# A hybrid encoder trunk on one core: norm sums of squares inside the output projections, roots with tokens on partitions, and one convolution operation per tap

## The chip, the cores and the metric

The kernel runs on one core of a Trainium2 chip. The metric is device time in microseconds (us) of one execution; the time of a kernel is the median of its runs.

## What is computed

Four layers act on a residual stream x of 768 tokens (a prompt of 512 and a sample of 256, independent streams that share weights) with 1024 channels, in fp32. Layers 0 and 3 mix with RWKV-7, layer 1 with Hyena long convolutions, layer 2 with a Conformer convolution module; a final norm ends the trunk.

```python
def rmsnorm(x, g):
    y = xf * lax.rsqrt(jnp.mean(xf * xf, axis=-1, keepdims=True) + RMS_EPS)
    return (y * g).astype(x.dtype)
def conformer_conv_mixer(h, w_in, dw_w, dw_b, ln_g, ln_b, w_out):
    a, b, g = jnp.split(h @ w_in, 3, axis=-1)
    u = a * jax.nn.sigmoid(b)
    u = depthwise_conv(u, dw_w, dw_b)              # 31 taps, per channel
    u = jax.nn.silu(layernorm(u, ln_g, ln_b))
    return (u * jax.nn.silu(g)) @ w_out
def trunk(...):
    for i in range(DEPTH):
        shift, scale, gate = ...                   # from silu(c) @ mod_w[i] + mod_b[i]
        hn = rmsnorm(x, norm_g[i]) * (1 + scale) + shift
        o = mixer(hn)                              # ends in @ w_out
        x = x + (gate * o)
    return rmsnorm(x, final_g)
```

## The kernel before

Channels lie on the 128 partitions, in eight tiles of 128 (KT = 8, index k or j); tokens lie along the free dimension, in two halves of 384 (h = 0 and 1). BX holds the residual, BH the normed input h, BD the residual times the root's inverse (and later scratch), BY the gated mixer output, SQ two 768-column scratch tiles. PSUM has eight banks: PJ (0, 1) for products, SC (2, 3), and IV, IU, SQB, YB (4 to 7). Each engine has its own program, written by hand and in order; semaphores join them.

A layer runs so. The **norm** (`norm` on PE, ACT and DVE): ACT squares each of the eight tiles (L1342), PE multiplies each square by a 128x128 matrix of 1/1024 (MEAN), which sums over channels and spreads the sum over all partitions (L982, 8 x 2 products of 384 columns); ACT takes the root of 768 columns (L1347), DVE its reciprocal (L1917), then x times it for eight tiles (BD, L1925); ACT scales and shifts into BH (L1357), a piece for the prompt and a piece for the sample. Before its first square, ACT waits for the last store of the residual to DRAM. Then comes the **mixer**. Its first weights and constants are loaded by SP after the whole of BH is there in layers 1 and 2; in layers 0 and 3 DVE first builds shifted differences of all of BH (L1945 to L1949). Then the **output projection** (`out_act`, `out_dve`, and the loop on PE, L949): eight products of 16 matmuls each, back to back on PE; DVE adds each to the old residual (L1433), which ACT has brought from DRAM two tiles at a time into SQ, and ACT stores the new one.

In layer 0 the norm stands beside the first modulation rounds on PE (`mod_rounds`, L627), which wait for 512 KB weight loads.

In the **conformer** PE makes three products a channel tile (slots b, a, g, in that order, banks CB[0] to CB[2], one buffer each); ACT takes a tanh of b and of g; DVE makes the gated input CU (L1649), then the gate BY (L1655), then 31 taps (L1668, L1671), each one operation for the prompt's 512 columns and one for the sample's 256, and a closing operation into BD (L1674).

Of the kernel before, what the change touches and what calls it, by code (L numbers as in the profile page):

```python
# [17 lines left out]
D = 1024  # L18
# [36 lines left out]
NV_CF = CONV + 3  # L55
NV_HY = 14
# [53 lines left out]
PER = {"act": {"gate": 0}, "dve": {"mod": 0, "gates": 0, "gate": 0, "pair": 73, "hy": 188, "cf": 64, "out": 0}}  # L110


def trunk_program(nc, a, out, layers=(0, 1, 2, 3)):
# [9 lines left out]
    with ctx:  # L123
# [18 lines left out]
        XO = SQ  # L142
# [12 lines left out]
        SEL = sb("SEL", [P, 2])  # L155

# [37 lines left out]
        CACC = own("CACC", [P, 2, T])  # L194
# [18 lines left out]
        alone.close()  # L213

# [22 lines left out]
        xn_ready, h_ready, hn_done = sem("xn_ready"), sem("h_ready"), sem("hn_done")  # L237
# [71 lines left out]
        for l in layers:  # L309
            phase((l, "norm"), 0, (), 1)  # L310
# [14 lines left out]
        phase(("final", "norm"), 0, (), 1)  # L325
# [70 lines left out]
        def tiles_hy(sp, l, load, free, cols):  # L396
# [3 lines left out]
            def one(j, first):  # L400
# [3 lines left out]
                for s, grp in enumerate((2, 0, 1, 3)):  # L404
                    load(s, cols(a["hy_w_in"][0], j + grp * KT), free[s] if first else (pj_full[1], j * 4 + (base + s - 3)))
                    if first and s == 0:
                        sp.wait_ge(h_ready, KT * (NRM[l] + 1))
# [18 lines left out]
        def _(sp):  # L426
# [30 lines left out]
            for l in layers:  # L457
                if l % 3 == 0:
# [16 lines left out]
                    def pair(j, first):  # L475
# [5 lines left out]
                        else:  # L481
                            sp.wait_ge(h_ready, KT * (NRM[l] + 1))
# [17 lines left out]
                if l % 3 == 2:  # L500
# [5 lines left out]
                    sp.wait_ge(h_ready, KT * (NRM[l] + 1))  # L506
# [289 lines left out]
        def pe_hyena(pe, l, product, weights, done):  # L796
# [4 lines left out]
            def project(j, s, halves=(0, 1)):  # L801
                weights((l, "hy"), s, j)
                for h in halves:
                    pe.wait_ge(pj_free[h], j * 4 + (base + s + 1))
                    for k in range(KT):
                        if type(j) is int and j == 0 and s == 0 and h == 0:
                            pe.wait_ge(h_ready, KT * NRM[l] + k + 1)
# [129 lines left out]
        def _(pe):  # L937
            pe.sem_inc(sq_used, 2)
# [32 lines left out]

            def norm(l):

                n, prods = NRM[l], plan[(l, "norm")][1]
                if n == 0:
                    pe.wait_ge(const_ready, 176)
                for k in range(KT):
                    pe.wait_ge(sq_ready, n * KT + k + 1)
                    for h in range(2):
                        if k == 0:  # L980
                            pe.wait_ge(pj_free[h], prods + 1)
                        mm = pe.matmul(pj(h), MEAN, SQ[:, k % 2, tok(h)], start=(k == 0), stop=(k == KT - 1))  # L982
                    mm.then_inc(sq_used, 1)

                pe.wait_ge(sq_used, n * KT + KT + 2)
                pe.sem_inc(pj_full[0], 1)
                pe.sem_inc(pj_full[1], 1)
# [5 lines left out]
            for l in layers:  # L993
                norm(l)
                if l == layers[0]:
                    pe.wait_ge(sc_ready, 1)
                    mod_rounds("mod", 0, MOD_FIRST)
# [23 lines left out]
                if l % 3 == 2:  # L1021
                    for j in range(0, KT):
                        for s in range(3):
                            weights((l, "cf"), s, j)
                            for h in range(2):

                                pe.wait_ge(cb_free[s][h], j + 1)
                                for k in range(KT):
                                    if s == 0 and h == 0:
# [1069 lines left out]
```

## Time and profile before

| | us |
|---|---|
| time, median of 3 runs (4233.78 to 4238.66) | 4234.78 |
| the profiled execution's own time | 4246.76 |
| its span, first to last instruction | 4245.0 |
| PE busy in it | 3499.3 (82%) |
| DVE busy | 2101.5 (50%) |
| ACT busy | 1136.3 (27%) |

The profiled execution is one run, 0.28% above the median. In the chain of work that ended last, followed back from the last instruction, PE has 31% of the span, DVE 9%, waiting that the profile doesn't explain 6%, ACT 1%, DMA under 1%. The mean granted TensorE clock is 0.895 of its full 2.4 GHz.

### The profile page before, as it was taken

Reading aid. Unit: us, or ns where it says so; the run is one execution under the profiler, and the core shown is the slowest. Engines: PE = TensorE matmul, PEld = TensorE weight load, DVE = VectorE, ACT = ScalarE, POOL = GpSimd, SP = SyncE. Lnnn points to the kernel's source line nnn. Section 1 sums busy time; section 2 is a strip of 40 time slices with the busy share of each in tenths; the row PEclk is TensorE's granted clock in tenths of the full one; section 3 lists DMA queues with packets and bytes.
Section 4 is the critical chain, followed back from the end, with each engine's and each line's share of the span. In section 5 each row is a group of like instructions: output and inputs, shape, how many; then the busy total and the mean of one; then the engine's idle time right before and its main releaser. Section 6 shows DMA issues by size and latency. Waiting matters only on the chain. (4 is left out here: it accounts for less than half of the span.)

```text
span 4245.0 us, 96984 instructions
## 1 busy us (share of the span) xinstructions
PE 3499.3 (82%) x41452; PEld 2472.3 (58%) x41452; DVE 2101.5 (50%) x4017; ACT 1136.3 (27%) x2764; POOL 0.2 (0%) x4
## 2 busy tenths in 40 slices
PE   4978888889888859899979797387788888888977
PEld 2556766676676526666655454144466666766664
DVE  3253454354444235767761599613545544454432
ACT  2132333333233113333320200101233333333320
POOL 0000000000000000000000000000000000000000
PEclk7989998888898979999989898698899989989988
DMA  3111111110110211111102111020000000000002
GB/s 141 55 62 41 54 45 34 48 63 27 38 62 32 88 69 32 38 30 45 30 20 80 51 45 45 8 92 30 27 18 8 18 17 13 13 13 18 16 24 93
DMA packets 65781, 178.67 MB, mean 42 GB/s; under 512 B 9104, under 2 KB 22544, under 8 KB 65424
## 3 DMA queue, kind: packets, MB, share of 16 engines
q1 hardware_dynamic: 53472, 144.02, 10.2%
q10 hardware_dynamic: 11952, 29.04, 1.9%
q8 instruction: 328, 5.37, 0.5%
q14 instruction: 29, 0.24, 0.0%
HBM read 157.30 MB, written 15.73 MB: 41 GB/s over the span
## 5 line engine op out<-in xcount | busy, mean ns | idle before, releaser
L1624 DVE SCALAR_TENSOR_TENSOR RBF<-bank,ID 128x256 bf16<-128x256 f32 x480 | 194.0, 423 | 402.7 <-PE bank L610 396.4
L949 PE MATMUL bank<-BY,W 128*128 128x384 f32 x1024 | 340.4, 496 | 48.0 <-DVEq L1697 35.3
L808 PE MATMUL bank<-BH,W 128*128 128x384 f32 x1024 | 341.6, 489 | 6.9 <-ACT HZ L1210 6.6
L949 PEld LDWEIGHTS bank<-BY,W 128*128 128x128 f32 x1024 | 198.7, 195 | 188.4 <-DVEq L1697 35.9
L1031 PE MATMUL bank<-BH,W 128*128 128x384 f32 x768 | 261.4, 505 | 38.2 <-DMA W<-in_cf_w_in 22.9
L949 PE MATMUL bank<-BX,W 128*128 128x384 f32 x640 | 219.1, 500 | 66.4 <-DVE BX L1936 66.1
L808 PEld LDWEIGHTS bank<-BH,W 128*128 128x128 f32 x1024 | 191.3, 191 | 136.3 <-issue 15.5
L1671 DVE SCALAR_TENSOR_TENSOR CACC<-CU,CV,CACC 128x512 f32<-128x512 f32 x480 | 254.7, 611 | 0.0
L1031 PEld LDWEIGHTS bank<-BH,W 128*128 128x128 f32 x768 | 151.2, 198 | 148.3 <-issue 29.8
L771 PE MATMUL bank<-BD,W 128*128 128x384 f32 x512 | 228.5, 575 | 0.0
L730 PE MATMUL bank<-BH,W 128*128 128x384 f32 x512 | 213.0, 546 | 8.9 <-DVE BH L1936 8.9
L949 PEld LDWEIGHTS bank<-BX,W 128*128 128x128 f32 x640 | 121.2, 193 | 163.7 <-issue 71.3
L1433 DVE SCALAR_TENSOR_TENSOR BX<-bank,MOD,SQ 128x384 f32 (+2 forms) x96 | 43.5, 481 | 301.0 <-PE bank L949 235.4
L730 PE MATMUL bank<-BX,W 128*128 128x384 f32 x512 | 181.2, 498 | 0.0
L610 PE MATMUL bank<-LN,Z 64*64 64x64 f32 x4608 | 163.7, 221 | 3.8 <-issue 3.8
L610 PEld LDWEIGHTS bank<-LN,Z 64*64 64x64 f32 x4608 | 149.0, 136 | 23.4 <-issue 23.4
L662 PE MATMUL bank<-VT,KS 64*64 64x64 f32 x1536 | 110.9, 239 | 44.7 <-ACTq L1133 26.6
L1342 ACT ACTIVATE SQ<-BX 128x768 f32<-128x768 f32 x40 | 33.2, 843 | 410.1 <-DMA x_scratch<-BX 376.1
L553 PE MATMUL bank<-BK,AR 64*64 64x64 f32 x1536 | 75.1, 268 | 73.8 <-DVE BK L1595 38.7
L1634 DVE TENSOR_TENSOR Z<-Z,bank 128x256 f32<-128x256 f32 x288 | 109.6, 418 | 52.8 <-PE bank L620 50.7
L730 PEld LDWEIGHTS bank<-BH,W 128*128 128x128 f32 x512 | 96.6, 204 | 66.3 <-issue 24.4
L620 PEld LDWEIGHTS bank<-ZB,RBF 64*64 64x64 bf16 x3840 | 95.0, 109 | 57.1 <-issue 52.7
(264 smaller groups left out, 6476.1 us busy)
## 6 DMA issues: line engine op xcount, KB each, us to landing
W<-in_mod_w SPq DMA_DIRECT2D x96, 512.0 KB, 3.6
W<-in_rw_w_in SPq DMA_DIRECT2D x68, 512.0 KB, 3.7
W<-in_hy_w_in SPq DMA_DIRECT2D x32, 512.0 KB, 7.0
x_scratch<-BX ACTq DMA_DIRECT2D x32, 384.0 KB, 3.4
W<-in_cf_w_in SPq DMA_DIRECT2D x24, 512.0 KB, 3.4
SQ<-x_scratch ACTq DMA_DIRECT2D x24, 384.0 KB, 4.2
W<-in_rw_w_out SPq DMA_DIRECT2D x16, 512.0 KB, 3.7
W<-in_hy_w_out SPq DMA_DIRECT2D x8, 512.0 KB, 3.5
```

The lines of the kernel that those rows point to most:

```text
L553: mm = pe.matmul(SC[1][rows, (d * GC + c) * CH:(d * GC + c + 1) * CH], AR[rows, p, d, c, 0, :], BK[rows, d, c, 0, :], start=True, stop=True)
L610: mm = pe.matmul(NB[d][rows, c * CH:(c + 1) * CH], lhs, rhs, start=True, stop=True)
L620: mm = pe.matmul(NB[d][rows, GT + c * CH:GT + (c + 1) * CH], RBF[rows, d, c, :], ZB[rows, d, c, :], start=True, stop=True)
L662: mm = pe.matmul(SQB[rows, o], KS[rows, p, d, c, 0, :], VT[rows, SGS[s][d] * GC + c, :], start=True, stop=not state)
L730: mm = pe.matmul(pj(h), W[:, s, k, :], src[:, k, tok(h)], start=(k == 0), stop=(k == KT - 1))
L771: mm = pe.matmul((SQB, YB)[h][:, 0:HALF], W[:, 2, k, :], BD[:, k, tok(h)], start=(k == 0), stop=(k == KT - 1))
L808: mm = pe.matmul(pj(h), W[:, s, k, :], BH[:, k, tok(h)], start=(k == 0), stop=(k == KT - 1))
L949: mm = pe.matmul(pj(h), lhs(k), rhs(k, h), start=(k == 0), stop=(k == nk - 1))
L1031: mm = pe.matmul(CB[s][h][:, 0:HALF], W[:, s, k, :], BH[:, k, tok(h)], start=(k == 0), stop=(k == KT - 1))
L1624: v.scalar_tensor_tensor(RBF[:, d, :, :], xout(d), -1.0, bc(ID2[:, 1 if r < NBF else 0, :], GC), ALU.mult, ALU.add).then_inc(ir_ready, 1)
L1634: v.tensor_tensor(z, z, uout(d), ALU.add).then_inc(z_ready, 1)
L1671: ins = v.scalar_tensor_tensor(dst, src, w, dst, ALU.mult, ALU.add)
```

## The change

In every output projection ACT squares each residual tile as DVE finishes it, a half at a time, and PE sums the squares there: for a square tile it loads each 128-token piece as the weights and multiplies it by one column of MEAN, so that the sums come out with tokens on partitions, three columns a half in SC. Each tile's sums follow the next tile's product in PE's order. The norm that follows takes roots and reciprocals of 128x3 elements a half (RN), lays them out as a diagonal pattern (RX, then SQ), and one product a half with MEAN spreads them over the partitions into SQB and YB. DVE's multiply into BD and ACT's scaling into BH then go by halves, with semaphores counted a half. The old residual comes into a buffer of its own (XOUT: TW, HZ or CACC by layer), two tiles ahead; a square root of one element at the start of the projection has ACT's table loaded there; the wait for the last store stands ahead of BH. In layer 0 the sums are taken up front, and PE's first modulation rounds wait until all of BD is made.

In the conformer a tap is one operation over 798 columns (both streams and the padding between them), in two accumulators in turn, which a closing pair of operations adds. The halving that the closing operation did is put into the tap weights once. The gate is made ahead of tap 12.

```diff
             with C.loop("cf", KT) as j:
...
+            C.link(v.tensor_scalar(CVA[:, :, 0:CONV], CVA[:, :, 0:CONV], 0.5, None, ALU.mult))
...
                 for tap in range(CONV):
-                    for st, (t0, ln) in enumerate(STREAMS):
-                        src = CU[:, starts[st] - PADW + tap:starts[st] - PADW + tap + ln]
-                        dst = CACC[:, 0, t0:t0 + ln]
-                        w = CV[:, tap:tap + 1]
-                        if tap == 0:
-                            ins = v.tensor_scalar(dst, src, w, None, ALU.mult)
-                        else:
-                            C.wait(last[st])
-                            ins = v.scalar_tensor_tensor(dst, src, w, dst, ALU.mult, ALU.add)
-                        last[st] = C.mark(ins)
+                    if tap == GATE_TAP:
+                        for h in range(2):
+                            v.wait_ge(cf_tanh, j * 2 + h + 1)
+                            v.scalar_tensor_tensor(BY[:, bass.ds(j, 1), tok(h)].squeeze(1), TT[:, 1, tok(h)], 1.0, CB[2][h][:, 0:HALF],
+                                                   ALU.add, ALU.mult).then_inc(cb_free[2][h], 1)
+                    b = tap % 2
+                    src, dst, w = CU[:, tap:tap + T + 2 * PADW], CACC[:, b, :], CV[:, tap:tap + 1]
+                    if tap < 2:
+                        ins = v.tensor_scalar(dst, src, w, None, ALU.mult)
+                    else:
+                        C.wait(last[b])
+                        ins = v.scalar_tensor_tensor(dst, src, w, dst, ALU.mult, ALU.add)
+                    last[b] = C.mark(ins)
...
+            def squares(n, k):
+                for h in range(2):
+                    pe.wait_ge(sq_ready, n * 2 * KT + 2 * k + h + 1)
+                    for c in range(3):
+                        t = h * HALF + c * P
+                        mm = pe.matmul(SC[h][:, c:c + 1], SQ[:, k % 2, t:t + P], MEAN[:, 0:1], start=(k == 0 and c == 0), stop=(k == KT - 1 and c == 2))
+                    mm.then_inc(sq_used, 1)
             def norm(l):
-                for k in range(KT):
-                    pe.wait_ge(sq_ready, n * KT + k + 1)
...
+                for h in range(2):
+                    pe.wait_ge(dg_ready, n * 2 + h + 1)
+                    pe.matmul((SQB, YB)[h][:, 0:HALF], MEAN, SQ[:, 0, tok(h)], start=True, stop=True).then_inc(r_full, 1)
...
                         done(product(i * 4 + (base + s), lambda k: W[:, s, k, :], lambda k, h: BY[:, k, tok(h)], KT), s)
+                        if i * 4 + s:
+                            squares(NRM[l] + 1, i * 4 + s - 1)
+                squares(NRM[l] + 1, KT - 1)
...
+            act.activation(RN[:, 0, 0:1], EPSV[:, 0:1], ACT.Sqrt)
+            for j in range(-2, KT):
+                if j >= 0:
                     for h in range(2):
                         act.wait_ge(pj_free[h], j + (base + 2))
+                        act.wait_ge(sq_used, (n + 1) * 2 * KT + 2 * j + h + 1)
+                        act.activation(SQ[:, j % 2, tok(h)], BX[:, j, tok(h)], ACT.Square).then_inc(sq_ready, 1)
+                    act.dma_start(a["xs"][n][j * P:(j + 1) * P, :], BX[:, j, :]).then_inc(x_out, 16)
+                if j + 2 < KT:
+                    act.dma_start(xo[:, j % 2, 0:T], src[(j + 2) * P:(j + 3) * P, :]).then_inc(xo_in[j % 2], 16)
...
+                    act.activation(RN[:, h, :], SC[h][:, 0:3], ACT.Sqrt, bias=EPSV[:, 0:1]).then_inc(rt_ready, 1)
...
+                        for k in range(KT):
+                            act.wait_ge(xn_ready, n * 2 * KT + h * KT + k + 1)
+                            for t0, t1, st in (((0, HALF, 0),) if h == 0 else ((HALF, LP, 0), (LP, T, 1))):
...
-                C.link(v.reciprocal(RS[:, :], RS[:, :]))
+                    v.wait_ge(rt_ready, n * 2 + h + 1)
+                    C.link(v.reciprocal(RN[:, h, :], RN[:, h, :]))
+                    C.link(v.scalar_tensor_tensor(RX[:, h, :, :], bc(RN[:, h, :], 2, 2), float(D), bc(HSUM[:, 0:P:HEAD], 3), ALU.mult, ALU.mult))
+                    v.tensor_tensor(SQ[:, 0, tok(h)].rearrange("p (x e) -> p x e", e=HEAD), bc(RX[:, h, :, :].rearrange("p c x -> p (c x)"), HEAD, 2),
+                                    bc(ID2[:, 0, :], 6), ALU.mult).then_inc(dg_ready, 1)
```

How PE's order moves is seen at the end of layer 1 and the start of layer 2. Before, PE's program there has Hyena's last inverse transform (INV), the output projection (BY with weights W), the norm's sums (SQ with the constant matrix K) and the conformer's input products (BH):

```order
L837 MATMUL bank<-INV,UP 128x128 x12
L949 MATMUL bank<-BY,W 128x384 x128
L982 MATMUL bank<-SQ,K 128x384 x16
L1031 MATMUL bank<-BH,W 128x384 x384
L949 MATMUL bank<-BD,K 128x384 x16
```

Now, at the end of the same projection (its first two products, 32 matmuls, stand ahead of the first six sums, and each later product of 16 is followed by six):

```order
L950 MATMUL bank<-BY,W 128x384 x16
L979 MATMUL bank<-K,SQ 128x1 x6
L950 MATMUL bank<-BY,W 128x384 x16
L979 MATMUL bank<-K,SQ 128x1 x12
L991 MATMUL bank<-SQ,K 128x384 x2
L1036 MATMUL bank<-BH,W 128x384 x384
```

The sixteen 384-column sums became 48 one-column ones, of which 36 stand inside the projection and 12 behind it, and two 384-column products are left between those and the next layer.

DVE's order in the conformer's loop, for one channel tile, was this before (CU the gated input, BY the gate, CACC the accumulator; two more operations for each of the 30 later taps):

```order
L1649 SCALAR_TENSOR_TENSOR CU<-SQ,bank 128x256
L1654 ISA
L1655 ISA
L1655 SCALAR_TENSOR_TENSOR BY<-SQ,bank 128x384
L1654 REGISTER_ALU
L1655 ISA
L1655 SCALAR_TENSOR_TENSOR BY<-SQ,bank 128x384
L1668 TENSOR_SCALAR CACC<-CU,CV 128x512
L1668 TENSOR_SCALAR CACC<-CU,CV 128x256
L77 REGISTER_ALU
L1671 SCALAR_TENSOR_TENSOR CACC<-CU,CV,CACC 128x512
```

Now the taps follow CU at once, and the gate stands in their midst:

```order
L1651 SCALAR_TENSOR_TENSOR CU<-SQ,bank 128x256
L1668 TENSOR_SCALAR CACC<-CU,CV 128x798 x2
L78 REGISTER_ALU
L1671 SCALAR_TENSOR_TENSOR CACC<-CU,CV,CACC 128x798
```

```order
L1671 SCALAR_TENSOR_TENSOR CACC<-CU,CV,CACC 128x798
L1662 ISA
L1663 ISA
L1663 SCALAR_TENSOR_TENSOR BY<-SQ,bank 128x384
L1662 REGISTER_ALU
L1663 ISA
L1663 SCALAR_TENSOR_TENSOR BY<-SQ,bank 128x384
L78 REGISTER_ALU
L1671 SCALAR_TENSOR_TENSOR CACC<-CU,CV,CACC 128x798
```

The first of these two pieces is the start of a channel tile, the second the place ahead of tap 12; sixty operations for the later taps became 29, and the gate's two moved behind twelve taps.

## Rows read from the trace of the kernel before

**Rows 1.** Timeline, layer 1's projection to layer 2: start us, us, engine, line, operation, [idle<-releaser].
```profile
2236.08 85.00 PE L949 MATMUL bank<-BY,W 128*128 128x384 f32 x256 [4.76 <-DVEq L1858]
...
2321.23 0.74 DVE L1433 SCALAR_TENSOR_TENSOR BX<-bank,MOD,SQ 128x128 f32 x2 [4.43 <-PE bank L949]
...
2325.49 12.28 PE L982 MATMUL bank<-SQ,K 128*128 128x384 f32 x32 [4.42 <-ACT SQ L1342]
...
2345.41 7.04 DVE L1925 TENSOR_TENSOR BD<-BX,YA 128x768 f32<-128x768 f32 x8
2346.41 9.70 ACT L1357 ACTIVATE BH<-BD,MOD,GS 128x512 f32<-128x512 f32 x16 [6.11 <-DVE BD L1925]
...
2360.66 39.73 PE L1031 MATMUL bank<-BH,W 128*128 128x384 f32 x113 [22.88 <-DMA W<-in_cf_w_in]
```

**Rows 2.** Timeline, end of layer 0's projection and of the norm behind it.
```profile
1517.73 1.45 PE L949 MATMUL bank<-BY,W 128*128 128x384 f32 x4
...
1543.20 9.69 ACT L1357 ACTIVATE BH<-BD,MOD,GS 128x512 f32<-128x512 f32 x16 [6.11 <-DVE BD L1925]
```

**Rows 3.** Timeline, the same two ends between layers 2 and 3.
```profile
2751.34 85.08 PE L949 MATMUL bank<-BY,W 128*128 128x384 f32 x256 [35.27 <-DVEq L1697]
...
2864.32 9.69 ACT L1357 ACTIVATE BH<-BD,MOD,GS 128x512 f32<-128x512 f32 x16 [6.11 <-DVE BD L1925]
```

**Rows 4.** Timeline, the last projection and the output's stores.
```profile
4119.01 85.60 PE L949 MATMUL bank<-BY,W 128*128 128x384 f32 x256 [3.99 <-DVEq L1497]
...
4235.27 6.29 ACTq L1417 DMA_DIRECT2D y<-BH  x8
```

**Rows 5.** Timeline, the conformer's first channel tile on DVE.
```profile
2384.70 0.62 DVE L1649 SCALAR_TENSOR_TENSOR CU<-SQ,bank 128x128 f32<-128x128 f32 x2 [4.68 <-PE bank L1031]
...
2396.28 0.75 DVE L1668 TENSOR_SCALAR CACC<-CU,CV 128x512 f32<-128x512 f32 x2
```

**Rows 6.** Timeline, one later channel tile on DVE.
```profile
2430.17 0.18 DVE L1641 COPY CV<-CVA 128x34 f32 x1 [0.65 <-DVE BD L1674]
...
2431.57 1.01 DVE L1655 SCALAR_TENSOR_TENSOR BY<-SQ,bank 128x384 f32 x2
...
2433.39 31.84 DVE L1671 SCALAR_TENSOR_TENSOR CACC<-CU,CV,CACC 128x512 f32<-128x512 f32 x60
...
2465.35 0.62 DVE L1674 TENSOR_SCALAR BD<-CACC,CV 128x768 f32 x1
2466.63 0.18 DVE L1641 COPY CV<-CVA 128x34 f32 x1 [0.66 <-DVE BD L1674]
```

**Rows 7.** Timeline, layer 0: the same DVE operation at 768 columns.
```profile
89.32 7.52 DVE L1936 SCALAR_TENSOR_TENSOR BX<-BD,MU,BH 128x768 f32<-128x768 f32 x8
```

**Rows 8.** Timeline: two-column products with 128x128 weights, in layers 1 and 3.
```profile
1644.33 1.84 PE L915 MATMUL bank<-K,HAS 128*128 128x2 f32 x16
...
3175.30 2.34 PE L710 MATMUL bank<-K,SQ 128*128 128x2 f32 x12 [2.12 <-ACT SQ L1171]
```

**Rows 9.** Windows: us, busy (count) of PE, PEld, DVE, ACT, POOL, clock, DMA, GB/s.
```profile
2236.00:2321.00 85.00, 84.92 (x256) 49.65 (x256) 10.14 (x22) 0.00 (x0) 0.00 (x0) 0.97 0.27 94
```

**Rows 10.** Groups by line and shape on ACT: count | busy us, mean ns | idle.
```profile
L1357 ACT ACTIVATE BH<-BD,MOD,GS 128x512 f32<-128x512 f32 x32 | 25.6, 801 | 21.1 <-DVE BD L1925 18.3 <-DVEq L1929 2.8
...
L1357 ACT ACTIVATE BH<-BD,MOD,GS 128x256 f32<-128x256 f32 x32 | 18.7, 585 | 0.0
```

**Rows 11.** Timeline, a root of 12 columns on ACT, layer 3.
```profile
4110.69 0.27 ACT L1174 ACTIVATE RT<-bank,EPSV 128x12 f32<-128x12 f32 x1 [1.51 <-PE bank L710]
```

**Rows 12.** Timeline, layer 0's norm and modulation rounds.
```profile
16.92 12.99 PE L982 MATMUL bank<-SQ,K 128*128 128x384 f32 x32 [16.92 <-ACT SQ L1342]
...
43.38 3.64 PE L627 MATMUL bank<-W,CTE 128*32 128x128 f32 x64 [9.11 <-DVE MOD L1902]
...
50.20 2.13 PE L627 MATMUL bank<-W,CTE 128*32 128x128 f32 x32 [0.40 <-DVE MOD L1902]
...
65.97 9.67 ACT L1357 ACTIVATE BH<-BD,MOD,GS 128x512 f32<-128x512 f32 x16 [2.78 <-DVEq L1929]
```

More of the change, by code:

```diff
@@ L106, in __exit__ @@
         c.n = 0
-PER = {"act": {"gate": 0}, "dve": {"mod": 0, "gates": 0, "gate": 0, "pair": 73, "hy": 188, "cf": 64, "out": 0}}
+PER = {"act": {"gate": 0}, "dve": {"mod": 0, "gates": 0, "gate": 0, "pair": 73, "hy": 188, "cf": 34}}
 def trunk_program(nc, a, out, layers=(0, 1, 2, 3)):
@@ L970, in mod_rounds @@
                     mm.then_inc(mod_sel, 1)
+            def squares(n, k):
[5 more added lines that the diff above has]
+                    mm.then_inc(sq_used, 1)
             def norm(l):
-                n, prods = NRM[l], plan[(l, "norm")][1]
+                n = NRM[l]
                 if n == 0:
                     pe.wait_ge(const_ready, 176)
-                for k in range(KT):
-                    pe.wait_ge(sq_ready, n * KT + k + 1)
[L979 to L987, printed above, removed]
+                    for k in range(KT):
+                        squares(0, k)
+                for h in range(2):
+                    pe.wait_ge(dg_ready, n * 2 + h + 1)
+                    pe.matmul((SQB, YB)[h][:, 0:HALF], MEAN, SQ[:, 0, tok(h)], start=True, stop=True).then_inc(r_full, 1)
             def done(mm, s):
@@ L1353, in norm @@
                         act.wait_ge(gs_ready, 1)
-                    for k in range(KT):
-                        act.wait_ge(xn_ready, n * KT + k + 1)
-                        for st, (t0, ln) in enumerate(STREAMS):
-                            ins = act.activation(BH[:, k, t0:t0 + ln], BD[:, k, t0:t0 + ln], ACT.Identity, scale=GS[:, k, st:st + 1],
-                                                 bias=MOD[:, l * 24 + k, st:st + 1])
-                        ins.then_inc(h_ready, 1)
+                    else:
+                        act.wait_ge(x_out, 16 * KT * n)
+                    for h in range(2):
+                        for k in range(KT):
+                            act.wait_ge(xn_ready, n * 2 * KT + h * KT + k + 1)
+                            for t0, t1, st in (((0, HALF, 0),) if h == 0 else ((HALF, LP, 0), (LP, T, 1))):
+                                ins = act.activation(BH[:, k, t0:t1], BD[:, k, t0:t1], ACT.Identity, scale=GS[:, k, st:st + 1],
+                                                     bias=MOD[:, l * 24 + k, st:st + 1])
+                            ins.then_inc(h_ready, 1)
             for l in layers:
@@ L1675, in dve_conformer @@
+                for st, (t0, ln) in enumerate(STREAMS):
+                    o = t0 + 2 * PADW * st
+                    t = C.mark(v.scalar_tensor_tensor(BD[:, bass.ds(j, 1), t0:t0 + ln].squeeze(1), CACC[:, 0, o:o + ln], CV[:, CONV:CONV + 1],
+                                                      CACC[:, 1, o:o + ln], ALU.add, ALU.add))
+                C.wait(t)
                 v.sem_inc(cf_conv, 1)
```

117 lines of the change are left out of this document (50 added, 67 removed).

## The prediction, as put on record before the changed kernel ran

> **What bounds the kernel now.** The table's shares come first: PE is busy 82% of the span and leads the chain of waits, so PE's work and its waits are what the time is made of; but an average over four layers says nothing about single stretches, so I read the timeline at each place that the diff touches. At a layer's end [rows 1] the reader sees PE run its projection without a pause until 2321.08 (2236.08 + 85.00), then DVE's last residual piece, then the norm: PE's sums, DVE's multiply, ACT's scaling until 2356.11, each engine waiting for the one before, and PE's next product at 2360.66, 39.6 us after the last one. None of this lies beside other work. From the projection's end to the end of BH the norm takes 35.0 us there; the same difference is 33.7 us ahead of layer 1 (1519.18 to 1552.89) [rows 2] and 37.6 us ahead of layer 3 (2836.42 to 2874.01) [rows 3]. The last norm and its stores take 40.4 us from 4204.60 to the span's end at 4245.0 [rows 4]. Inside the conformer DVE sets the beat: one channel tile takes 36.46 us (2430.17 to 2466.63) and DVE is hardly ever idle in it [rows 6], while PE needs 96 records x 0.332 = 31.9 us a tile (0.332 from the 256 records in 85.00 us of [rows 1]).
>
> **The shorter norm.** I call T0 the end of PE's eighth product and build the new chain from rows. DVE's last residual piece ends at T0 + 0.15 + 0.74 = 0.9 [rows 1]. ACT squares 384 columns: the line through 801 ns at 512 and 585 ns at 256 gives 692 at 384 for an operation with scale and bias [rows 10]; a square has neither, I take 0.55, so 1.5. PE meanwhile does tile 6's sums, then tile 7's, done at 2.8 (prices below). The root of three columns costs at most the 0.27 of twelve [rows 11]: 3.1. DVE's reciprocal and its spreading are small operations, 0.18 each by the 34-column copy [rows 6], plus a wait on itself between them, and the diagonal's multiply of 384 columns is about 0.5, half of the 768-column multiply (7.04 / 8 = 0.88) [rows 1] and a little; half 0, whose sums end 0.7 earlier, has its diagonal at 3.6 and half 1 at 4.6. PE's product with MEAN is two records of 0.332 with a load and its way out, 0.9: 4.6 and 5.5. DVE then makes BD by halves, 16 operations of some 0.47, and ACT follows one behind from about 5.3. ACT is the slower: overlapping as now (16 pieces in 9.70 us where their means add to 11.1, so 0.09 each) [rows 1, 10], eight pieces of 384 take 0.60 each and eight pairs of 128 and 256 take 0.39 + 0.49, together 11.8, which ends BH at T0 + 17.1. What ACT waits for there beside DVE is the last store, issued at 1.5; a store of this size is on the way some 2 to 4 us by the pause between the last residual piece and the first sums now (2321.97 to 2325.49) [rows 1], so it is there at about 5.3 too.
> So the three inner norms go from 33.7 + 35.0 + 37.6 = 106.3 to 3 x 17.1 = 51.3: 55.0 saved. What follows (weight loads behind the whole of BH, DVE's differences) keeps its length. At the end, DVE makes the output itself in 16 operations of about 0.53 from T0 + 5.5, done at 14.0; the last store goes out by 14.6 and lands as now 3.4 later (4235.27 + 6.29 = 4241.56 to 4245.0) [rows 4]: 18.0 for 40.4, saved 22.4. Sum 77.4.
>
> **What the projections pay.** PE has no gap there (84.92 us busy of 85.00 at a granted clock of 0.97) [rows 9], so each record of the sums adds its whole time. A block is six matmuls, twelve records, each loading 128x128 and multiplying one column. The nearest rows are products of two columns with such a load: 16 records in 1.84, 0.115 each, right behind other products, and 12 in 2.34, 0.195 each, after PE had idled 2.12 us [rows 8]. Inside a projection PE doesn't idle, so I take 0.115: 1.38 a block and 0.1 for the change back, 1.5. The ends are 1.2 (some loads hidden behind the product ahead) and 2.45. Six blocks stand ahead of T0 in each of four projections: 24 x 1.5 = 36.0 (29 to 59). Net of these, the norms bring 41.4. The old residual's earlier load and ACT's early table load bring nothing of their own: PE doesn't wait for the one, and the other is within the chain that I have built anew.
>
> **The conformer.** A 768-column operation with a scalar pointer goes at 7.52 / 8 = 0.94, 0.93 without the last one's end [rows 7]; a pair of 512 and 256 takes 31.84 / 30 = 1.06 [rows 6], so a further operation costs 0.13 and a column 1.04 ns, and 798 columns take 0.13 + 0.83 = 0.96 (0.98 if all of 0.94 grew with the columns; 0.90 if the 0.13 halved). The 29 later taps take 28 x 0.96 + 1.05 = 27.9 for 31.84, saved 3.9. The first two taps are two operations of 0.55 (under the 0.62 of 768 columns [rows 6]), and with the gate, moved among the taps at 0.93, the stretch from 2431.57 to 2433.39 grows from 1.82 to 2.25. The closing pair is 0.66 + 0.48 for 0.62. A tile goes from 36.46 to 33.5. In the first tile the taps now begin when CU is made (2384.70 + 0.62, and a wait of 0.14) rather than behind the gate at 2396.28 [rows 5]: 10.8 earlier; twelve taps take 10.7, about when the tanh that the gate needs is there, so that wait is gone and not just moved. All told: 10.8, 2.0 in the first tile, 7 x 2.96 in the others, 33.6 saved.
> What waits for the gate is PE: its third product of the next tile now waits for a bank that comes free some 12.9 us into DVE's tile. PE has by then done the second product (10.6 from 0.6 on), so it waits about 2 us, and its tile is 31.9 + 2 = 33.9 at most against DVE's 33.5. But DVE needs that product only 20 us later, so a lag is taken up; I cost it at nothing, and at 8 x 0.4 to 8 x 1.5 if the lag did not level off.
>
> **Layer 0** loses. The sums run up front: 96 records, some two blocks slow as the first products are now (12.99 us for 32 from 16.92 on) [rows 12], the rest at 0.115, end at about 29.8, as now; 0.195 throughout would end them at 35.6. The chain above then needs 9.2 to the last of BD: 39.1. PE's first modulation round waits for that; now it runs ahead and the second one begins at 43.38, after 9.11 us of waiting for DVE. A round lasts 6.82 (43.38 to 50.20), so the second begins at 45.9, and its weights, whose loads wait for the first round, may add 0.7: 2.5 to 3.2 late, carried to the scaling at 65.97, which itself takes 11.8 for 9.67. Loss 5.7, up to 12.
>
> **The sum:** 41.4 + 33.6 - 5.7 = 69.3 us, so 4246.76 - 69.3 = 4177.5 for the profiled execution. It lies 0.28% above the median, so the same ratio, 0.9837, gives 4234.78 x 0.9837 = 4166 for the median.
>
> **Rivals.** *The sums cost the slow price:* 2.45 a block in the projections and about a microsecond more in each norm, 27 us, so 4193; for it speaks that nothing here shows one-column products; against it that PE comes to them without a pause.
> *PE becomes the conformer's bound:* the gate's wait and slow stretches after it add 1.5 us a tile, 12 us: 4178. For it speaks how close 33.9 and 33.5 lie; against it the 20 us of slack.
> *More is saved:* blocks at 1.2 (7 us), taps at 0.90 (14 us at most), layer 0 even (6 us): taken by halves, 4152.
> *Slower:* the changes between products and sums act on PE as pauses, and its clock falls from 2.4 to 1.2 GHz after each. If the half product behind a block then ran at the lower level, 16 records would take 5.3 more, a block 1.0 more: 24 x 6.3 = 151, so 4317. It cancels all from 69.3 / 24 = 2.9 us more a block. The second row of [rows 8] speaks for it (0.195 after an idle), the first against it (0.115 for small products with none). The Trainium skill's page "TensorE: Matmul & The Clock Gate", section "A second HAM failure mode: psum-queue depth-cycling", says that brief idling of PE between groups of matmuls can make the clock swing between its levels; by that rule the time would be that of this rival, by the rows that of the forecast, and the trace agrees only as far as the 0.195 after an idle goes.
>
> **How the numbers follow.** Forecast 0.60; the slow price 0.15; PE as bound 0.07; more saved 0.13; the falling clock 0.05, of which 0.03 beyond the break-even and 0.02 near it. The predicted time is the forecast's, 4166. The norm chain is built of some ten small steps, good to 1.5 us in each of four places, which with the ends above gives the forecast its own 4156 to 4178; the range 4148 to 4190 adds most of the three next cases. A difference of under 0.2%, about 8 us, can't be told from none; faster by more is 0.95, the same 0.02, slower 0.03.
>
> **What would show it.** From the end of the last projection product to the end of BH about 17 us in layers 1 to 3; blocks of 12 records in 1.4 us in each projection, with the granted clock still at 0.97, and a projection of 94 instead of 85; conformer tiles of 33.5 with DVE never waiting at the gate; the first BH of layer 0 some 3 us later. The prediction is wrong if a block takes over 2 us, if matmuls behind a block take 0.64 instead of 0.33 a record, if a tap takes over 1.0, or if DVE stands still ahead of tap 12.

## The result, and the profile after

The changed kernel takes 4169.18 us (median of 4 runs, 4165.6 to 4177.09), the kernel before 4234.28 on the same chip (4232.8 to 4238.66): a ratio of 0.9847, 95% interval 0.983 to 0.9864, so 65.1 us faster. The forecast was 4166 and the range 4148 to 4190. The profiled execution of the changed kernel took 4168.61 us, 78 less than that of before (4246.76), because the one of before was a long one; the first experiment below shows where that came from.

The table sets the traces against each other, stretch by stretch as TensorE (PE) bounds them in its timeline.

| stretch, us | before | after | difference | forecast |
|---|---|---|---|---|
| start to the first gate product | 90.5 | 101.8 | +11.3 | +5.7 |
| layer 0's mixer | 1344.0 | 1334.3 | -9.7 | 0 |
| four output projections | 340.4 | 372.5 | +32.1 | +36.0 |
| four norms, from a projection's last product to PE's next, the last to the end | 178.2 | 100.9 | -77.3 | -77.4 |
| conformer, first product to its layernorm | 324.2 | 289.3 | -34.9 | -33.6 |
| Hyena, layer 3's mixer, layernorm | 1967.7 | 1968.0 | +0.2 | 0 |
| span | 4245.0 | 4166.8 | -78.2 | -69.3 |

The four stretches that the change touches give 77.3 + 34.9 - 32.1 - 11.3 = 68.8. Layer 0's mixer, which it doesn't touch, gives the other 9.7.

First the page of the changed kernel.

```profile
span 4166.8 us, 96873 instructions
PE 3494.4 (84%) x41792; PEld 2497.7 (60%) x41792; DVE 2059.9 (49%) x3835; ACT 1151.6 (28%) x2840; POOL 0.2 (0%) x4
```

PE is busy 5 us less than before, ACT 15 more, in a span 78 us shorter: for these two, what went is waiting, and not work. DVE is busy 42 us less, 31 of it in the later taps (L1671, 254.7 us before and 224.1 now); in the conformer, where DVE sets the beat, it is work that went. The timeline of PE in layer 0's projection (start us, us, engine, line, operation, [idle before <-what ended it]):

```profile
1458.75 1.40 PE L979 MATMUL bank<-K,SQ 128*128 128x1 f32 x12
1460.01 10.57 PE L950 MATMUL bank<-BY,W 128*128 128x384 f32 x32
1470.41 1.40 PE L979 MATMUL bank<-K,SQ 128*128 128x1 f32 x12
```

A block of twelve records (six matmuls, of which the trace shows two records each) takes 1.40, and the next product starts 1.26 after the block did. The product behind it goes at 10.57 / 32 = 0.330 a record, as before (0.332) [rows 1]: its clock didn't fall. The same kernel at the end of layer 1, which answers to [rows 1]:

```profile
2319.61 4.03 PE L950 MATMUL bank<-BY,W 128*128 128x384 f32 x12
...
2323.48 2.73 PE L979 MATMUL bank<-K,SQ 128*128 128x1 f32 x24
2323.68 0.74 DVE L1435 SCALAR_TENSOR_TENSOR BX<-bank,MOD,HZ 128x128 f32<-128x128 f32 x2 [4.47 <-PE bank L950]
2324.46 0.52 ACT L1081 ACTIVATE SQ<-BX 128x384 f32<-128x384 f32 x1 [4.69 <-DVE BX L1435]
...
2326.25 0.26 ACT L1349 ACTIVATE RN<-bank,EPSV 128x3 f32<-128x3 f32 x1 [0.41 <-PE bank L979]
...
2326.97 2.53 PE L991 MATMUL bank<-SQ,K 128*128 128x384 f32 x4 [0.75 <-DVE SQ L1924]
...
2328.22 7.52 DVE L1937 TENSOR_TENSOR BD<-BX,bank 128x384 f32<-128x384 f32 x16 [0.42 <-PE bank L991]
2328.86 11.90 ACT L1361 ACTIVATE BH<-BD,MOD,GS 128x384 f32<-128x384 f32 x24 [2.35 <-DVE BD L1937]
...
2345.09 3.27 PE L1036 MATMUL bank<-BH,W 128*128 128x384 f32 x5 [15.60 <-DMA W<-in_cf_w_in]
```

The last product ends at 2323.64 and BH at 2340.76, so 17.1 us for the 35.0 of before; the long pieces are still ACT's scaling and, behind BH, the weights' load. In the conformer, VectorE (DVE) shows the first channel tile and the start of the next two; they answer to [rows 5, 6]:

```profile
2367.50 0.62 DVE L1651 SCALAR_TENSOR_TENSOR CU<-SQ,bank 128x128 f32<-128x128 f32 x2 [4.67 <-PE bank L1036]
2368.22 1.18 DVE L1668 TENSOR_SCALAR CACC<-CU,CV 128x798 f32<-128x798 f32 x2
...
2378.93 1.01 DVE L1663 SCALAR_TENSOR_TENSOR BY<-SQ,bank 128x384 f32 x2
2379.86 18.33 DVE L1671 SCALAR_TENSOR_TENSOR CACC<-CU,CV,CACC 128x798 f32<-128x798 f32 x19
...
2400.18 0.18 DVE L1643 COPY CV<-CVA 128x34 f32 x1 [0.64 <-DVE BD L1677]
...
2433.73 0.18 DVE L1643 COPY CV<-CVA 128x34 f32 x1 [0.63 <-DVE BD L1677]
```

The taps start right behind CU, the gate (L1663) has no idle time ahead of it, and a tile lasts 33.55 (2400.18 to 2433.73). Layer 0, last, is where the change loses; [rows 12] are those of before:

```profile
16.58 20.61 PE L979 MATMUL bank<-K,SQ 128*128 128x1 f32 x96 [16.58 <-ACT SQ L1346]
...
39.02 7.52 DVE L1937 TENSOR_TENSOR BD<-BX,bank 128x384 f32<-128x384 f32 x16 [0.53 <-PE bank L991]
...
46.63 3.64 PE L628 MATMUL bank<-W,CTE 128*32 128x128 f32 x64 [6.38 <-issue]
...
52.66 1.35 PE L628 MATMUL bank<-W,CTE 128*32 128x128 f32 x32 [0.43 <-DVE MOD L1907]
...
75.19 11.89 ACT L1361 ACTIVATE BH<-BD,MOD,GS 128x384 f32<-128x384 f32 x24 [2.78 <-DVEq L1941]
...
101.80 6.52 PE L950 MATMUL bank<-BX,W 128*128 128x384 f32 x14 [27.47 <-DVE BX L1948]
```

The sums end at 37.19 where the forecast had 29.8, and every later step carries that delay.

### The profile page after: what moved, and what is told of

It reads as the page before. It is cut to its first block and busy times, and to the rows that moved or that the text cites. A ratio compares the mean times of both kernels' runs of the same rounds, so it can differ in the third digit from the quotient of the medians.

```text
span 4166.8 us, 96873 instructions
## 1 busy us (share of the span) xinstructions
PE 3494.4 (84%) x41792; PEld 2497.7 (60%) x41792; DVE 2059.9 (49%) x3835; ACT 1151.6 (28%) x2840; POOL 0.2 (0%) x4
## 5 line engine op out<-in xcount | busy, mean ns | idle before, releaser
L809 PE MATMUL bank<-BH,W 128*128 128x384 f32 x1024 | 342.1, 489 | 6.9 <-ACT HZ L1217 6.6
L1036 PE MATMUL bank<-BH,W 128*128 128x384 f32 x768 | 249.3, 488 | 15.6 <-DMA W<-in_cf_w_in 15.6
L1671 DVE SCALAR_TENSOR_TENSOR CACC<-CU,CV,CACC 128x798 f32<-128x798 f32 x232 | 224.1, 1042 | 0.0
L731 PE MATMUL bank<-BH,W 128*128 128x384 f32 x512 | 210.6, 541 | 8.9 <-DVE BH L1948 8.9
L621 PE MATMUL bank<-ZB,RBF 64*64 64x64 bf16 x3840 | 117.0, 194 | 15.4 <-DVE RBF L1625 12.2
L1081 ACT ACTIVATE SQ<-BX 128x384 f32<-128x384 f32 x64 | 33.5, 523 | 343.6 <-DVE BX L1435 343.6
```

Of the source, the lines that this page charges most:

```text
L621: mm = pe.matmul(NB[d][rows, GT + c * CH:GT + (c + 1) * CH], RBF[rows, d, c, :], ZB[rows, d, c, :], start=True, stop=True)
L731: mm = pe.matmul(pj(h), W[:, s, k, :], src[:, k, tok(h)], start=(k == 0), stop=(k == KT - 1))
L809: mm = pe.matmul(pj(h), W[:, s, k, :], BH[:, k, tok(h)], start=(k == 0), stop=(k == KT - 1))
L1036: mm = pe.matmul(CB[s][h][:, 0:HALF], W[:, s, k, :], BH[:, k, tok(h)], start=(k == 0), stop=(k == KT - 1))
L1671: ins = v.scalar_tensor_tensor(dst, src, w, dst, ALU.mult, ALU.add)
```

## The experiments

Ten runs follow. All times are medians against the kernel before on the same chip, except the first, a single run. Edits are shown against the changed kernel.

**The kernel before, profiled once more.** No edit. It asks whether layer 0's mixer was 9.7 us shorter because of the change.

> The kernel before, unchanged, profiled a second time. From the first profile of before to that of after, 78 us are gone, but only 65 by the medians, and about 10 of the 13 lie in layer 0 between its first gate product and its output projection, where the change has no instruction (1344.0 us then, 1334.3 in the profile of after). Theory: that first profile was a long one of its kind and the change does nothing there; this profile's stretch is then within 3 us of 1334 and its span near 4235. Rival: the change shortens that stretch (something shared, as code or buffers); it is then again near 1344.

It took 4226.3 us, span 4224.5. PE's first gate product starts at 89.29 and its projection at 1418.12:

```profile
89.29 10.87 PE L949 MATMUL bank<-BX,W 128*128 128x384 f32 x27 [25.37 <-DVE BX L1936]
...
1418.12 7.21 PE L949 MATMUL bank<-BY,W 128*128 128x384 f32 x13 [4.00 <-DVEq L1497]
```

So the mixer took 1328.8 where the first trace of the same kernel had 1344.0. Both values are below the expected 1334 and 4235, and the mixer's is below that of the change too, so the rival, a change that shortens this stretch, falls. Over all traces of all kernels here it lies between 1328.5 and 1344.0, with not one of its instructions changed. The 9.7 us in the table are scatter, and single traces compare to about 15 us as a whole, but to about one within the stretch of a norm or a projection and two within the conformer.

**The convolution alone.** The norms and projections are those of the kernel before; the conformer is that of the change:

```diff
-                            squares(NRM[l] + 1, i * 4 + s - 1)
...
-                for h in range(2):
-                    pe.wait_ge(dg_ready, n * 2 + h + 1)
...
+                for k in range(KT):
+                    pe.wait_ge(sq_ready, n * KT + k + 1)
```

> The kernel before with the conformer's part of the change alone (one operation a tap, two accumulators, gate ahead of tap 12). Theory: this part brings the 33 to 35 us that the two traces show between the conformer's first input product and its layer norm (324.2 then, 289.3 now), whatever the norms do: 4200 us. Rival: part of it comes from the norm's change (PE starts the layer at another clock or the weights come earlier): then under 28 us is saved, over 4206.

4202.83 us (4197.54 to 4203.75), ratio 0.9922, 0.9906 to 0.9939; 31.1 us faster. The conformer's stretch is 291.05 in its trace (324.17 and 324.18 in the two of before); norms and projections are as before.

**The norms alone.** The conformer is that of the kernel before:

```diff
-                    src, dst, w = CU[:, tap:tap + T + 2 * PADW], CACC[:, b, :], CV[:, tap:tap + 1]
...
+                    for st, (t0, ln) in enumerate(STREAMS):
+                        src = CU[:, starts[st] - PADW + tap:starts[st] - PADW + tap + ln]
```

> The change without its conformer part (two operations a tap, gate ahead of the taps, as before). Theory: the norms' four shorter chains bring 77 us, the sums in the projections take 32 and layer 0 takes 11, so 34 us are left: 4200 us. Rival: the parts are not additive (the projections' sums or layer 0 disturb clocks and loads elsewhere): 4210 or more, or under 4190.

4203.07 us (4198.94 to 4206.6), ratio 0.9923, 0.9907 to 0.994; 30.8 us faster. The two parts add: 31.1 + 30.8 = 61.9, beside 65.1 for the whole, with runs of one kernel some 5 us apart. In this trace projections (93.0 to 93.5), norms and layer 0 (first gate product at 102.03) stand as in the change.

**Every sum in the projections taken twice.** The second set goes into columns that nobody reads. It asks what a one-column record costs at twice the number:

```diff
...
+                    for c in range(3 if n else 0):
+                        t = h * HALF + c * P
+                        mm = pe.matmul(SC[h][:, 4 + c:5 + c], SQ[:, k % 2, t:t + P], MEAN[:, 0:1], start=False, stop=(k == KT - 1 and c == 2))
```

> The change with each block of sums in the output projections made twice (the second time into columns that nothing reads; layer 0's own norm as it is). Theory: a record of the sums costs its 0.105 us and nothing behind it, so 32 more blocks of 12 records cost 32 x 1.26 = 40 us: 4209 us. Rival (the falling clock): a longer interruption of the products lowers PE's clock behind it; then products behind a block show 0.64 us a record and the time is 4240 or more.

4235.95 us (10 runs, 4225.66 to 4244.14), ratio 1.0003, 0.9993 to 1.0014: the whole gain gone, 27 us above the 4209 expected and somewhat under the rival's 4240. PE's timeline in layer 0's projection:

```profile
1454.61 0.72 PE L979 MATMUL bank<-K,SQ 128*128 128x1 f32 x6
1455.19 0.81 PE L982 MATMUL bank<-K,SQ 128*128 128x1 f32 x6
1455.86 0.81 PE L979 MATMUL bank<-K,SQ 128*128 128x1 f32 x6
1456.53 0.93 PE L982 MATMUL bank<-K,SQ 128*128 128x1 f32 x6
1457.32 12.13 PE L950 MATMUL bank<-BY,W 128*128 128x384 f32 x32
```

The block of 24 records takes 2.71 (1454.61 to 1457.32), about what was expected, but the product behind it takes 12.13 where the change has 10.57. The slow price of [rows 8] for the 384 further records, 384 x 0.195 = 75 us, would come to much the same time, but it isn't what happened: no block in the four projections takes over 2.94, 0.12 a record. The windows show what did, the block itself first (window; us, busy time and count of PE, PEld (PE's weight loads), DVE, ACT, POOL; granted clock; DMA share; GB/s):

```profile
1454.60:1457.30 2.70, 2.70 (x25) 2.69 (x24) 0.74 (x2) 0.53 (x1) 0.00 (x0) 0.96 0.40 111
1457.30:1462.00 4.70, 4.70 (x11) 2.73 (x12) 0.00 (x0) 0.00 (x0) 0.00 (x0) 0.66 0.55 215
1462.00:1466.00 4.00, 4.00 (x14) 2.35 (x13) 0.62 (x1) 0.52 (x1) 0.00 (x0) 1.00 0.00 0
1525.80:1530.00 4.20, 4.20 (x10) 2.46 (x11) 0.00 (x0) 0.00 (x0) 0.00 (x0) 0.65 0.00 1
```

For the first 4 us or so behind some of the blocks, the granted clock is 0.65 of 2.4 GHz on the mean, so most of that stretch is at 1.2, though PE had not paused for a moment. Not every block does it: in the four projections the product behind 11 of the 24 blocks takes 12.0 to 13.6, behind the other 13 the 10.57 of the change. The norms lose as well, 2.0 to 4.3 us each: they begin with 48 such records in a row, of which the last six take 1.30 behind layer 0's projection, for the 0.81 within a block.

**The gate ahead of the taps.** It asks whether the first tile's wait is gone or only hidden by the place of the gate:

```diff
-GATE_TAP = 12
+GATE_TAP = 0
```

> The change with the conformer's gate ahead of the first tap again (its place before), all else as changed. Theory: in the first channel tile DVE then waits for PE's third product and its tanh, as before, and the taps begin some 11 us later; in the later tiles nothing changes, since PE never waited for the gate's bank: 4180 us. Rival: the gate's place also sets PE's pace (a bank free earlier or later): 4169 or under 4175.

4187.19 us (4182.16 to 4191.03), ratio 0.9882, 0.9865 to 0.9898: 18 more than the change in its first comparison, where 11 were expected. DVE in the first tile:

```profile
2375.78 0.62 DVE L1651 SCALAR_TENSOR_TENSOR CU<-SQ,bank 128x128 f32<-128x128 f32 x2 [4.67 <-PE bank L1036]
...
2386.66 0.56 DVE L1663 SCALAR_TENSOR_TENSOR BY<-SQ,bank 128x384 f32 x1 [4.60 <-ACT SQ L1400]
2387.14 1.18 DVE L1668 TENSOR_SCALAR CACC<-CU,CV 128x798 f32<-128x798 f32 x2
```

The first tap starts 10.7 us behind CU (2376.40 to 2387.14) instead of 0.1, and the conformer's stretch is 302.09, 12.8 longer. So the gate's place alone is worth that, nearly all of it in the first tile; the rest of the 18 is not in the conformer (layer 0's mixer, which scatters, is 5 us longer in this trace than in the change's).

**128 columns in layer 0's sums.** Each square's load is then followed by a product of 128 columns of MEAN, every one with the same sum, of which the root reads one:

```diff
-                        mm = pe.matmul(SC[h][:, c:c + 1], SQ[:, k % 2, t:t + P], MEAN[:, 0:1], start=(k == 0 and c == 0), stop=(k == KT - 1 and c == 2))
+                        w = P if n == 0 else 1
+                        mm = pe.matmul(SC[h][:, c * w:(c + 1) * w], SQ[:, k % 2, t:t + P], MEAN[:, 0:w], start=(k == 0 and c == 0), stop=(k == KT - 1 and c == 2))
...
```

> The change with layer 0's sums made against 128 equal columns of the matrix instead of one (same weights loads, same results in every 128th column); the other norms as changed. In the trace of the change these 96 records take 20.6 us, 0.214 each to the end, where the 384-column ones before took 0.64 for some 5 us and 0.32 after that. Theory: with the one-column products PE's clock does not rise, with 128 columns it does after some 5 us: the sums take about 14 us, and 6 to 7 us are saved: 4162 us. Rival: the pace is that of the loads of weights there, whatever the columns: 20 us again, 4169.

4157.49 us (4149.7 to 4162.96), ratio 0.9807, 0.9791 to 0.9824.

```profile
16.84 13.06 PE L980 MATMUL bank<-K,SQ 128*128 128x128 f32 x96 [16.84 <-ACT SQ L1347]
30.65 1.79 PE L992 MATMUL bank<-SQ,K 128*128 128x384 f32 x4 [0.75 <-DVE SQ L1925]
...
94.49 5.75 PE L950 MATMUL bank<-BX,W 128*128 128x384 f32 x9 [27.48 <-DVE BX L1949]
```

128 times the columns, and the 96 records take 13.06 us instead of 20.61. The first gate product comes 7.3 us earlier than in the change. The one-column sums of layer 0 were not slow by their number or by ACT's squares; they were slow for as long as PE did nothing but one-column products. The trace's own record of the clock says the same: here its first entry is a rise to 2.4 GHz at 21.2 us, where the records go from 0.214 to 0.112 each; in the change's trace the first entry is at 40.5, when the sums are over.

**An earlier first modulation round.** In layer 0 the spread roots go into another bank, so that PE's rounds needn't wait until DVE has read it for all of BD:

```diff
-                    pe.matmul((SQB, YB)[h][:, 0:HALF], MEAN, SQ[:, 0, tok(h)], start=True, stop=True).then_inc(r_full, 1)
+                    pe.matmul((SQB if n else IU, YB)[h][:, 0:HALF], MEAN, SQ[:, 0, tok(h)], start=True, stop=True).then_inc(r_full, 1)
...
-                    pe.wait_ge(xn_ready, 2 * KT)
...
```

> The change with layer 0's roots spread into another bank, so that PE's first modulation round need not wait until DVE has made all of BD. Theory: the round starts at about 40 instead of 46.6 us, its weights' successors are loaded earlier, and the scaling of layer 0 starts 5 to 6 us earlier: 4164 us. Rival: the rounds are paced by their weight loads, or by DVE's additions behind BD, in any case: under 2 us, 4168.

4169.92 us (4165.06 to 4171.89), ratio 0.9845, 0.9828 to 0.9861.

```profile
41.45 2.96 PE L628 MATMUL bank<-W,CTE 128*32 128x128 f32 x64
...
96.66 4.18 PE L950 MATMUL bank<-BX,W 128*128 128x384 f32 x6 [27.48 <-DVE BX L1947]
```

In the trace the first round starts at 41.45 instead of 46.63 and the first gate product at 96.66 instead of 101.80, so 5.1 us are there, as the theory had it. The median, with runs 7 us apart, shows none of it; the traced run is the shortest of the four, and what the others did at the start is not on record.

**Twice the sums, 128 columns each.** The experiment of the doubled sums with wide products, the second set into two banks that are free there:

```diff
-                        mm = pe.matmul(SC[h][:, c:c + 1], SQ[:, k % 2, t:t + P], MEAN[:, 0:1], start=(k == 0 and c == 0), stop=(k == KT - 1 and c == 2))
+                        mm = pe.matmul(SC[h][:, c * P:c * P + (P if n else 1)], SQ[:, k % 2, t:t + P], MEAN[:, 0:P if n else 1], start=(k == 0 and c == 0), stop=(k == KT - 1 and c == 2))
+                    for c in range(3 if n else 0):
+                        t = h * HALF + c * P
+                        mm = pe.matmul((IV, IU)[h][:, c * P:(c + 1) * P], SQ[:, k % 2, t:t + P], MEAN[:, 0:P], start=(k == 0 and c == 0), stop=(k == KT - 1 and c == 2))
...
```

> As the kernel with the sums twice in every projection (4236 us, where 4209 was expected; its trace shows products behind a block slow for some 4 us, at a granted clock of 0.58 to 0.66, though PE never paused, and the last block's sums at 0.21 a record), but both sets against 128 columns instead of one; layer 0's own norm as changed. Theory: what PE does in the block lets the clock fall, one-column products more than 128-column ones; now products behind a block keep 0.33 a record, and the cost is the records alone, 32 x 12 x 0.118 and 32 x 12 x 0.013 for the first set, 51 us: 4220. Rival: any 2.8 us between two products lets the clock fall: 4245 or more.

4203.78 us (4202.02 to 4210.29), ratio 0.9928, 0.9911 to 0.9945: 32 us faster than the same number of one-column sums, and 16 less than expected. A block and the product behind it, and the granted clock there:

```profile
1454.35 0.83 PE L979 MATMUL bank<-K,SQ 128*128 128x128 f32 x6
...
1457.03 10.49 PE L950 MATMUL bank<-BY,W 128*128 128x384 f32 x32
```

```profile
1457.00:1461.00 4.00, 4.00 (x15) 2.41 (x15) 0.00 (x0) 0.00 (x0) 0.00 (x0) 1.00 0.67 265
```

The 24 records take 2.68, as long as 24 of one column (the expectation had priced them higher), and the clock is whole behind them; behind all 24 blocks of the four projections the product takes 10.49. So a record with a 128x128 load costs the same for 1 and for 128 columns, and only behind the one-column blocks did the clock fall. The second set lies in other banks here, so the width is not the only difference between these two kernels; the next one has the banks of the change.

**Both remedies, in every norm.** 128 columns everywhere, and layer 0's earlier round:

```diff
-                        mm = pe.matmul(SC[h][:, c:c + 1], SQ[:, k % 2, t:t + P], MEAN[:, 0:1], start=(k == 0 and c == 0), stop=(k == KT - 1 and c == 2))
+                        mm = pe.matmul(SC[h][:, c * P:(c + 1) * P], SQ[:, k % 2, t:t + P], MEAN[:, 0:P], start=(k == 0 and c == 0), stop=(k == KT - 1 and c == 2))
...
-                    pe.wait_ge(xn_ready, 2 * KT)
...
-                    act.activation(RN[:, h, :], SC[h][:, 0:3], ACT.Sqrt, bias=EPSV[:, 0:1]).then_inc(rt_ready, 1)
+                    act.activation(RN[:, h, :], SC[h][:, 0:3 * P:P], ACT.Sqrt, bias=EPSV[:, 0:1]).then_inc(rt_ready, 1)
...
```

> This kernel is the change with two edits: every norm's sums are taken against 128 columns instead of one, and layer 0's first modulation round uses a bank that is free, so that TensorE does not wait there for the modulated tiles. Theory (layer 0's stretch is two costs in a row, the sums at half speed and the first modulation round behind a wait; a 128-column sum costs no more than a one-column one): the first gate product starts 7 + 5 = 12 us earlier, at about 90 instead of 101.8; the projections stay at 93 us and the inner norms at 30, 21.5 and 32, since the products of the first 12 records are not slower; time about 4157 us, against 4169 for the change on the same chip. Rival 1 (the two edits save the same wait, on W's loads: what one gains the other cannot): the first gate product starts no earlier than 94.5, time about 4162. Rival 2 (128 columns cost TensorE more behind the products than in layer 0, where nothing else runs): projections 97 and more, time about 4175.

4148.88 us (4144.21 to 4161.33), ratio 0.9799, 0.9785 to 0.9814: the lowest median here, where 4157 was expected. It is clear of the earlier round alone; against 128 columns in layer 0 alone (0.9807, 0.9791 to 0.9824) the intervals overlap, and it is the trace that sets the two apart.

```profile
16.64 13.53 PE L979 MATMUL bank<-K,SQ 128*128 128x128 f32 x96 [16.64 <-ACT SQ L1345]
30.93 1.79 PE L991 MATMUL bank<-SQ,K 128*128 128x384 f32 x4 [0.76 <-DVE SQ L1923]
32.65 1.95 PE L628 MATMUL bank<-W,CTE 128*32 128x128 f32 x64
...
88.01 20.16 PE L950 MATMUL bank<-BX,W 128*128 128x384 f32 x53 [27.48 <-DVE BX L1947]
...
2308.70 2.84 PE L979 MATMUL bank<-K,SQ 128*128 128x128 f32 x24
...
2312.29 1.79 PE L991 MATMUL bank<-SQ,K 128*128 128x384 f32 x4 [0.75 <-DVE SQ L1923]
```

The first gate product starts at 88.01, earlier than in the kernel before (90.48 and 89.29): what layer 0 lost is all won back, and the two remedies don't save the same wait. The projections stay at 92.9 to 93.5. In the inner norm between layers 1 and 2 the product with MEAN takes 1.79 where the change has 2.53, behind the same number of sums in the same banks (2.84 us for 2.73) and the same pause of 0.75. The granted clock over these products, in the change and here:

```profile
2327.00:2329.60 2.60, 2.50 (x4) 0.77 (x4) 2.11 (x6) 0.74 (x2) 0.00 (x0) 0.59 0.00 0
```

```profile
2312.30:2314.90 2.60, 1.78 (x4) 0.58 (x4) 2.41 (x7) 1.01 (x2) 0.00 (x0) 1.00 0.00 0
```

So the width of the sums alone decides here whether the clock falls behind 24 of them.

**The change again**, unaltered, on the chip of the kernel just told.

> The change as it is, once more on the chip of the run beside it. Theory: the two parts and layer 0 stay where they were, the first gate product at 102, the projections 93, the inner norms 30, 21.5 and 32, the conformer 289 to 291; 4169 us. Rival (part of the first trace's gain was scatter of layer 0's mixer stretch, 1329 to 1344 us in the runs so far): the median stays at 4169 and the span moves with that stretch alone, by up to 8 us.

4166.8 us (4163.12 to 4170.44), ratio 0.9835, 0.9822 to 0.9849; first gate product at 102.36, projections 92.9 to 93.4, inner norms 29.44, 21.51 and 32.21, conformer 290.87, layer 0's mixer 1334.6. The gain against the kernel before is 68.9 here and 65.1 in the first comparison. The kernel with both remedies is 17.9 us ahead of it on the same chip, with no run of the one among those of the other; by the traces 14.3 of that lie ahead of the first gate product and 1.9 in the norms.

## Why the prediction was right, step by step

The mechanism held, and the sum of the touched stretches, 68.8 by the trace, came out at the 69.3 of the forecast because two of its terms were off by some 4 to 6 us in opposite directions: that the total came so close was luck.

**The norm chain** was right to the microsecond: 17.1 to 17.6 from the last product to the end of BH at the three inner norms (forecast 17.1), 17.2 at the end (18.0). The one small step that was short is the product with MEAN: 0.9 a half was forecast, and both halves took 2.53 to 2.93 together, because they run behind 24 one-column records, at a granted clock of 0.59 where it was read, between layers 1 and 2; with 128 columns they took 1.79, there at 1.00.

**The block's price** was slightly too high: 1.5 was taken, and a projection grew by 7.8 to 8.3 for six blocks, so 1.3 to 1.4 each. The lower row of [rows 8], 0.115 a record, was the right one to go by (1.40 / 12 = 0.117). The rival of the slow price, 0.195, did not happen there.

**The falling clock** did not happen between the products of the change's projections: all 24 products behind a block take 10.57. It did happen at their ends: behind the last 24 records it made the product with MEAN the longer one just told. The doubled sums show how near the rival was: behind 24 one-column records in a row the clock falls at 11 places of 24. The mechanism that the rival gave was wrong, though. It had the changes between products and sums act as pauses. PE makes none there, 2.70 us busy out of 2.70 in the block and 4.70 out of 4.70 behind it, at a granted 0.66; the block with 128 columns, as long and with as many changes, leaves the clock at 1.00, and in the norms, with the banks the same as well, it is again the width alone that decides. The Trainium skill's page "TensorE: Matmul & The Clock Gate", section "A second HAM failure mode: psum-queue depth-cycling", names brief idling between groups of matmuls as what makes the clock swing, in a kernel that goes through PSUM banks in turn; the trace here agrees with a swing, but not with idling as its cause.

**Layer 0's loss** was mis-sized: 5.7 forecast, 11.3 measured. (The prediction's own terms, a delay of 2.5 to 3.2 and 2.1 of longer scaling, come to 4.6 to 5.3 and not to 5.7.) The step that failed is "the rest at 0.115": the sums were to speed up after two blocks, and all 96 went at 20.61 / 96 = 0.215. That alone made BD and the rounds 7 us later than forecast; the second round starts at 52.66 (forecast 45.9), BH at 75.19, and the scaling's 11.89 for 9.67 adds 2.2 (forecast 2.1). The other price on record, 0.195 throughout, would have ended the sums at 35.6, nearer to the 37.2 that they took. The same rows that gave the right price in the projections gave the wrong one here: there one-column records stand between wide products, here they stand alone. The upper end that was kept, 12, covered it.

**The conformer** was right in each term: the first tile's taps begin 0.10 behind CU, a tap takes 18.33 / 19 = 0.965 (forecast 0.96), a tile 33.55 (33.5). The saving of 10.8 + 2.0 + 7 x 2.9 is 33.1, as the convolution alone shows (324.2 to 291.05); 289.3 in the change's own trace is the short end of 289.3 to 291.1 over the traces. The one statement that failed cost nothing: PE was to wait some 2 us a tile for the gate's bank. It never does, as this window over its products shows (PE 248.91 us busy of 249.00):

```profile
2345.00:2594.00 249.00, 248.91 (x768) 146.54 (x768) 219.99 (x265) 24.20 (x38) 0.00 (x0) 0.99 0.15 52
```

The forecast put PE and DVE in step, but PE's tile (249.34 us of timeline / 8 = 31.2) is shorter than DVE's, and DVE starts two products behind it. PE draws ahead by 2.4 a tile, and worked out from these rows its last third product, at 2345.09 + 7.67 x 31.17 = 2584.1, still finds the gate of the tile before made at 2378.93 + 6 x 33.55 + 1.01 = 2581.2. Three more microseconds of lead, or two more tiles, and it would wait; DVE, which bounds the stretch, would not notice.

## What to carry to other kernels

A reduction that hangs on a long chain (sum, root, spread, scale) can be worth moving into a matmul stage that is already full: there every record of its sums is paid in full (32 us over four projections here), but the chain behind loses more (77 us), if only a few columns are left for the root and the reciprocal; what remains is the scaling itself. Take such sums against 128 columns, and not one: in these runs 128 columns cost nothing and kept the clock (other widths were not run). When a step is moved to the front of a stage, ask what its price was measured beside, because the same record cost 0.117 us between wide products and 0.215 alone.

## What the runs showed of the hardware that was not expected

- On products of one column TensorE stayed at half speed for 20 us without any pause. Layer 0's 96 one-column records took 0.215 us each to the last; the same loads with 128 columns took 13.06 / 96 = 0.136, the first ones slow included. In the window of the change's trace the granted clock nevertheless reads 1.00:

```profile
17.00:37.00 20.00, 20.00 (x95) 20.00 (x95) 0.62 (x3) 8.50 (x16) 0.00 (x0) 1.00 0.05 21
```

  The trace's record of the clock has no entry before 40.5 us there, and a stretch ahead of the first entry reads as whole. In the trace of the kernel before, the first entry, a rise at 21.8, stands where its 384-column records go from 0.64 to 0.32. Ahead of the first entry the record's duration tells the level, and the clock's column doesn't.
- 24 one-column records in a row (2.7 us) between wide products lowered the granted clock of the next 4 us to about 0.65 behind 11 blocks of 24 and not behind the others (why there and not elsewhere is open); 12 in a row (1.40 us) did it behind none of the change's 24 blocks, and 24 with 128 columns (2.68 us) behind none of theirs.
- A stretch without one changed instruction, layer 0's mixer of some 1330 us, differed by 15 us between executions. Where that comes from was not looked into; it may be why 5 us that a trace shows clearly are missing from a median of four runs.
